# Hybrid trunk kernel: other order of projections inside the attention heads of layer 1, value projection one step later in layer 0, and waits on exponential and root kept only where they share a PSUM bank

## What is computed

```python
qh = (rms_norm(cq, g_mla_q) @ w_mla_qb).reshape(B, T, MLA_HEADS, MLA_NOPE + MLA_ROPE)   # 8 heads, 64 + 32
kvh = (rms_norm(ckv, g_mla_kv) @ w_mla_kvb).reshape(B, T, MLA_HEADS, MLA_NOPE + MLA_V)  # 64 of keys, 128 of values
f['gqa_q'] = rope_2d(rms_norm(gq.reshape(B, T, GQA_HEADS, GQA_HD), g_gqa_q), tabs_gqa)  # 8 heads of 128, 2 of keys
s = jnp.einsum('bqhgd,bshd->bhgqs', qblk, kf) * scale
pr = jax.nn.softmax(s, axis=-1)
out = jnp.einsum('bhgqs,bshe->bqhge', pr, vf)
f['gates'] = gates.reshape(B, T, N_BRANCH, D_MODEL)   # 3 x 1024 columns of h @ w_in
```

## Time and profile before

| | |
|---|---|
| median of 3 runs | 3745.88 us (3745.24 to 3748.95) |
| the profiled execution, its own time | 3743.77 us |
| its span, first to last instruction | 3741.9 us |
| mean granted TensorE clock | 0.938 of 2.4 GHz |
| TensorE busy, matmuls | 3305.7 us (88%) |
| TensorE busy, weight loads | 2786.6 us (74%) |
| VectorE, ScalarE, GpSimd busy | 1550.6, 1281.4, 477.3 us (41%, 34%, 13%) |
| DMA | 297.11 MB, 79 GB/s |

### The profile page before, as it was taken

The page is one execution under the profiler, slowest core; times in us unless marked ns, Lnnn a source line. Parts: engine busy times, 40 slices in busy tenths (PEclk is TensorE's granted clock), DMA queues, the critical chain, the costliest instruction groups (busy, mean ns, idle before and its releaser), DMA issues.

```text
span 3741.9 us, 50235 instructions
## 1 busy us (share of the span) xinstructions
PE 3305.7 (88%) x18696; PEld 2786.6 (74%) x18696; DVE 1550.6 (41%) x1997; ACT 1281.4 (34%) x1778; POOL 477.3 (13%) x340
## 2 busy tenths in 40 slices
PE   6788897999999988799999967988798999879998
PEld 4678776888888876588888746777677777758886
DVE  4455423544334433422222245653455344453334
ACT  3344332444333332221211223443344333433222
POOL 2011100111000000300000130220011001021001
PEclk8888898999999999899999978999899999989999
DMA  4111141111321123124233231212111321223332
GB/s 159 55 43 56 38 124 40 61 56 60 115 65 62 53 91 128 51 63 133 73 95 107 96 124 54 68 59 84 56 58 61 99 64 62 82 93 100 93 99 95
DMA packets 91434, 297.11 MB, mean 79 GB/s; under 512 B 10320, under 2 KB 16592, under 8 KB 91344
## 3 DMA queue, kind: packets, MB, share of 16 engines
q1 hardware_dynamic: 55872, 202.40, 17.1%
q10 hardware_dynamic: 35472, 93.49, 7.6%
HBM read 274.88 MB, written 20.97 MB: 79 GB/s over the span
## 4 chain that ended last, share of the span: by engine, by line
PE 40%; issue 9%; DVE 6%; ACT 3%; DMA 3%; POOL 1%; ACTq 0%; DVEq 0%; POOLq 0%
PE ps L1278 37%; DMA mraw<-in_wmod 2%; DVE prob L1001 1%; PE ps L1366 1%; DVE mx L838 1%; PE ps L1344 1%; POOL ptl L1260 1%; ACT pth L437 1%; DVE tmp L983 0%; DVE tmp L817 0%; ACT wh L384 0%; DVE wl L807 0%; DVE ptl L856 0%; DVE xz L1165 0%; DVE tmp L877 0%
## 5 line engine op out<-in xcount | busy, mean ns | idle before, releaser
L1278 PE MATMUL ps<-hh,wh 128*128 128x512 f32 x2768 | 835.0, 362 | 123.0 <-POOL hl L1242 64.0
L1278 PE MATMUL ps<-hl,wh 128*128 128x512 f32 x2768 | 823.1, 358 | 0.0
L1278 PE MATMUL ps<-hh,wl 128*128 128x512 f32 x2768 | 820.5, 357 | 0.0
L807 DVE TENSOR_TENSOR wl<-raw,wh 128x1024 fp32r<-128x1024 f32 x364 | 481.9, 1324 | 696.8 <-ACT wh L384 669.3
L1278 PEld LDWEIGHTS ps<-hh,wh 128*128 128x128 f32 x2768 | 457.7, 192 | 223.9 <-issue 59.0
L1278 PEld LDWEIGHTS ps<-hh,wl 128*128 128x128 f32 x2768 | 458.5, 192 | 78.5
L1278 PEld LDWEIGHTS ps<-hl,wh 128*128 128x128 f32 x2768 | 459.9, 193 | 73.6
L384 ACT ACTIVATE wh<-raw 128x1024 fp32r<-128x1024 f32 x364 | 382.8, 1052 | 245.9 <-PE ps L1278 202.6
L1278 PE MATMUL ps<-yh,wh 128*128 128x512 f32 (+1 forms) x1296 | 410.2, 371 | 37.4 <-DVE yl L1132 17.1
L1278 PE MATMUL ps<-yl,wh 128*128 128x512 f32 (+1 forms) x1296 | 397.8, 361 | 0.0
L1278 PE MATMUL ps<-yh,wl 128*128 128x512 f32 (+1 forms) x1296 | 397.4, 361 | 0.0
(11 more groups left out here) (176 smaller groups left out, 3729.3 us busy)
## 6 DMA issues: line engine op xcount, KB each, us to landing
raw<-in_stream SPq DMA_DIRECT2D x364, 512.0 KB, 3.6
mraw<-in_wmod ACTq DMA_DIRECT2D x80, 512.0 KB, 3.7
gspill<-prob ACTq DMA_DIRECT2D x24, 384.0 KB, 2.3
tmp<-gspill ACTq DMA_DIRECT2D x24, 384.0 KB, 3.1
early<-in_wmod SPq DMA_DIRECT2D x16, 512.0 KB, 15.0
dec<-in_dec ACTq DMA_DIRECT2D x8, 768.0 KB, 4.2
gspill<-side ACTq DMA_DIRECT2D x24, 256.0 KB, 2.2
tmp<-gspill ACTq DMA_DIRECT2D x24, 256.0 KB, 2.7
```

The source lines that it names most:

```text
L807: dve.tensor_tensor(wl[:, s, :], raw[:, s, :], wh[:, s, :].bitcast(F32), ALU.subtract).then_inc(sem("w_lo"), 1)
L1278: ins = pe.matmul(out, lhs[w], rhs[x](cols), start=start and n == 0, stop=stop and n == 2)
```

## The change

Six edits:

1. `mla_steps`: with six tiles the values are projected in step 5, not 4; with four tiles the gate comes in step 0 and the query in step 1, not the other way round.
2. `mla_order` is new: it gives the place of query, gate and key/value chunk in a head's three chunks (query, gate, pair with six tiles; gate, query, pair with four; without a gate or without a query 0, 0, 1). Waits for `product` and `free0` use it. ScalarE and VectorE split a head's second chunk in step 0 and its third in step 1 in either case; the rotary step follows the query projection by one step, the query's split by two.
3. `stream_of`: the last layer's latent heads have their gate chunk ahead of the query chunk.
4. TensorE waits for `y_lo` only ahead of the scores of tiles 0 and 2, not of tile 4.
5. PV waits for the exponential of tile min(n, 2), not min(n, nq-2). With four tiles this is the same number.
6. The wait for `v_std` moves from the end of `fill(2)` to ahead of the score of tile 3, and is gone from the projections of the first grouped-query head, which no score follows at once.

```diff
@@ mla_steps, mla_order @@
-    return (0, (1, 2), 3, 4) if nq == 6 else (0, (1,), 2, 3)
+    return (0, (1, 2), 3, 5) if nq == 6 else (1, (0,), 2, 3)
+def mla_order(nq, gated):
+    return ((0, 1, 2) if nq == 6 else (1, 0, 2)) if gated else (0, 0, 1)
@@ ScalarE, mla_head @@
                 q, gs, k, v = mla_steps(nt // P)
-                ck = c0 + 1 + gated
+                iq, ig, ik = mla_order(nt // P, gated and query)
                 def fill(n):
+                    if query and n == 0:
+                        split(at, c0 + 1)
+                    if query and gated and n == 1:
+                        split(at, c0 + 2)
                     if query and n == q:
-                        split(at, c0 + 1)
-                        act.wait_ge(sem("product"), at.v("chunk", c0 + 1))
+                        act.wait_ge(sem("product"), at.v("chunk", c0 + iq + 1))
...
-                    if query and gated and n == gs[0]:
-                        split(at, ck)
                     if gated and n == gs[-1]:
-                        gate_out(at, c0 + query, f0 + query, kg, nt)
-                    if query and n == 2:
+                        gate_out(at, c0 + ig, f0 + ig, kg, nt)
+                    if query and n == q + 2:
...
@@ VectorE, mla_head @@
-                    if query and n == q:
+                    if query and n == 0:
                         split(at, c0 + 1)
-                    if query and n == 1:
-                        dve.wait_ge(sem("free0"), at.v("free0", f0 + 1))
+                    if query and n == q + 1:
+                        dve.wait_ge(sem("free0"), at.v("free0", f0 + iq + 1))
                         cosine(at, MLA_NOPE)
                         sine(at, kp, MLA_NOPE)
-                    if query and gated and n == gs[0]:
+                    if query and gated and n == 1:
                         split(at, c0 + 2)
-                    if query and n == 2:
+                    if query and n == q + 2:
                         query_lo(at, kp, par, nt)
@@ TensorE, attend and values @@
-                        if n % 2 == 0 and c.has(n - 5):
+                        if n in (0, 2) and c.has(n - 5):
                             pe.wait_ge(sem("y_lo"), c.v("y_lo", n // 2 - 3))
+                        if n == 3 and std is not None:
+                            pe.wait_ge(sem("v_std"), std)
...
-                pe.wait_ge(sem("s_exp"), c.v("s_exp", min(n, c.nq - 2)))
+                pe.wait_ge(sem("s_exp"), c.v("s_exp", min(n, 2)))
@@ TensorE, mla_head and gqa_query @@
-                        project(at, c0, 0, f0, R[0], RKT, nt, whole)
+                        project(at, c0 + iq, 0, f0 + iq, R[0], RKT, nt, whole)
                     if gated:
-                        gate(at, c0 + query, f0 + query, gs, n, nt)
+                        gate(at, c0 + ig, f0 + ig, gs, n, nt)
...
-                    if query and n == 2:
-                        pe.wait_ge(sem("v_std"), at.v("v_std", kq + 1))
@@ TensorE, the loops @@
-                            attend(t, k, 1 - k, nt, head(t, 3 * k, nf * k, k))
+                            std = t.v("v_std", k + 1) if kind == "gqa" else None
+                            attend(t, k, 1 - k, nt, head(t, 3 * k, nf * k, k), std=std)
@@ stream_of @@
+            if h and layer == DEPTH - 1:
+                gate(h - 1)
             put(split_rope(w["w_mla_qb"][layer][:, h * MLA_QK:(h + 1) * MLA_QK], MLA_NOPE))
-            if h:
+            if h and layer < DEPTH - 1:
                 gate(h - 1)
```

More of the change, by code:

```diff
@@ L488, in fill @@
                     if query and n == v:
-                        plain(at, ck, 0, vh[:, par, :])
+                        plain(at, c0 + ik, 0, vh[:, par, :])
                 return fill
@@ L1313, in stats, with attend @@
                 ins.then_inc(sem("v_stat"), 1)
-            def attend(at, ka, par, nt, fill=lambda n: None, first=False, last=False):
+            def attend(at, ka, par, nt, fill=lambda n: None, std=None, first=False, last=False):
                 c = Tiles(at, ka, nt // P, first)
@@ L1392, in mla_head @@
                 q, gs, k, v = mla_steps(nt // P)
-                ck, fk = c0 + 1 + gated, f0 + 1 + gated
+                iq, ig, ik = mla_order(nt // P, gated and query)
+                ck, fk = c0 + ik, f0 + ik
                 s = at.slot(ck)
@@ L1500, in _ @@
                     pe.wait_ge(sem("v_lo"), at.v("v_lo", 1))
-                    attend(at, 0, 0, nt, head(at, c1, f1, 1), first=True)
+                    std = at.v("v_std", 2) if kind == "gqa_first" else None
+                    attend(at, 0, 0, nt, head(at, c1, f1, 1), std=std, first=True)
                 elif kind in ("mla", "gqa"):
```

## The result

The changed kernel takes 3720.26 us (median of six runs, 3716.8 to 3726.0); the kernel before took 3745.56 us beside it. The ratio is 0.9933, with a 95% interval of 0.9919 to 0.9946: 0.67% faster. The forecast was 3724. The profiled execution took 3716.8 us, with a span of 3715.0.

The account below looks back on a forecast made before the run. TensorE is busiest in all attention stages, so time is won only where it waits or runs at half clock. -15.6 - 1.1 + 6.5 - 1.3 - 10 = -21.5 from 3743.8 gives 3722.3, 3724 for the median; range 3708 to 3741.

Parts of the forecast that it names:

- forecast -15.6 and -1.1: Layer 0 latent: seven heads gain 15.6 us as values cover step 5's wait; last head's PV starts 1.1 us earlier.
- Rival (b): Layer 0 latent: value projection stays at half clock behind PV, +15 instead of -15.6 us, kernel 3755; chance 0.07.
- rival (d): Layer 0, step 4: the exponential is not what it waits for; partly true, 1.1 us, in the sum; no separate chance.
- forecast +6.5 and -1.3: Layer 1 latent, gate first: seven heads lose 0.95 us each, +6.5; last head's gate fills step 0's wait, -1.3.
- forecast -10: Layer 1 grouped-query: root waited for before score 3 gains 10 us net of half clock; bounds -15.5 and -6.
- -15.5 of the forecast: Layer 1 grouped-query: six heads' gain without the root wait, 15.5 us, before the half clock charge of +5.5.
- forecast 0: Layer 0 grouped-query: neither removed wait ends last, as a 4.3 us gate piece intervenes; 0 within 1 us.
- Rival (a): Layer 0 and 1 attention heads: half clock behind the waits takes the gain, no change, 3745; chance 0.12.
- Rival (c): Waits fall so little work is at half clock: layer 0 -3.5 a head, grouped-query -15, kernel 3710; chance 0.15.

Follow-up runs that it names:

- e5: e1 with PV of step 4 waiting for exp(4) again: 3738.99 us, ratio 0.9982.
- e1: Kernel before with layer 0's part alone: values in step 5, PV waiting for at most exp(2), no `y_lo` wait in step 4: 3727.24 us.
- e6: e1 with the values back in step 4, so that only the waits are cut: 3740.28 us, ratio 0.9989.
- e7: The changed kernel with the `y_lo` wait of step 4 put back: 3721.67 us, ratio 0.9937.
- e3: Kernel before with only the root's wait moved ahead of score 3: 3733.51 us, ratio 0.9974.
- e8: e4 with layer 0's split of the next weight chunk moved from step 3 to step 4, behind tile 1: 3708.98 us.
- e10: e4 with layer 1's grouped-query query halves made earlier: high half ahead of exp(3), low half ahead of reciprocal and scale: 3697.25 us.
- e11: e10 with layer 0's whole key block, copy and split, moved to step 4: 3676.83 us, ratio 0.9822.
- e4: The changed kernel with layer 1's latent order put back to query first: 3716.66 us, ratio 0.9930.

## Why the prediction was right

**Layer 0, latent (forecast -15.6 and -1.1; stage -17.1).** The mechanism is right, and so is the size of each term. Wait 4.63 (4.7 forecast); stretch 15.4 us (15.3 + 0.15); seven stretches 123.72 - 107.63 = -16.1; `ptl` unmoved at +4.74; PV at half clock and the projection at full. In the last head the wait fell from 5.02 to 3.86, -1.16. The sum hides two small errors that cancel: outside the stretches the seven heads got 1.2 us longer, and the last head got 2.2 us shorter and not 1.1. Rival (b) needed the value projection at half clock behind PV, and it ran at 1.00. Its argument, that the projection never brings the clock back and PV does, is not what the trace shows: before the change the clock fell during the projection and came back 6.8 or 10.2 us later, after the change 3.4 or 6.8 us later, and what ran meanwhile doesn't tell the heads apart. That exp(4) was worth something only with the values moved (e5 less e1: 10.5 us) is rival (d) in its right size: the shorter wait alone, e6, is nothing.

**Layer 1, latent (forecast +6.5 and -1.3; stage +7.1).** With T the transposes at 2375.96, keys at T+7.08 (7.05 forecast), exp(2) at T+9.03 (8.95), PV at T+10.07 (10.0), next head at T+19.88 (19.9). Heads 28.6 instead of 28.8. The wait at the head's start was 0.82, not 1.3, since TensorE was ready that much later; by the timeline the head's length hung on VectorE. Two terms were mis-sized. The last head, given -1.3, takes 44.3 us after 44.2: its step 0 wait of 3.16 us went, but the one in step 2 grew from 3.52 to 4.07, and TensorE was busy at half clock for 15.6 us of that head after 11.0. The seven heads were given +6.5 at 0.95 each; six of them grew by 4.6 in all, 0.76 each, and the first by 2.5, so that +7.0 is close to the forecast by luck.

**Layer 1, grouped-query (forecast -10; stage -12.2).** From the maximum's start to the next score 3.98 us (3.97), and no wait for the root. Six heads went from 205.25 to 192.05 us, -13.2. The term that was mis-sized is the half clock at the new place: 0.9 us in each of six heads was taken, +5.5; it came in two of six, 2 x 1.6 = 3.2. Without it the six heads would have given -16.4, near the -15.5 of the forecast. The last head is 1.2 us longer with the half clock behind its own wait, and the first 0.3 shorter: -12.2 in all. The wait was 2.4 us, not 2.9. The Trainium skill (TensorE: Matmul & The Clock Gate, "HAM oscillation — how this bites in real kernels") tells of a kernel that waits 3 to 5 us in every turn of its loop and is throttled again each time. The waits here are shorter, and the trace shows half clock behind some of them all the same: behind 2.75 to 2.85 us in five heads of six before, behind 2.35 to 2.44 us in two of six now.

**Layer 0, grouped-query (forecast 0).** -2.6 inside a spread of 3.6 between profiles. With the `y_lo` wait put back (e7) the stage takes 335.4 us, with the root's wait alone moved (e3) 332.8, both inside that spread too.

**The sum.** -21.5 was forecast against the profiled execution; it came to -27.0, of which -22.2 (-17.1, +7.1, -12.2) are in the three stages that the sum is about, close to the -21.5. The other -4.8 are the spread of the profiles and no merit of the forecast. Rival (a) happened in a third of the heads of layer 1, at no cost in the latent ones, and left the value projections of layer 0 alone. Rival (c), 3710, was reached by no part of the change, but by e8, e10 and e11: it needed shorter waits, and these hung on VectorE's queue.

## What to carry to other kernels

A wait may grow and the kernel still win: what counts beside the idle time is how much work runs at half clock behind it. Here two waits of 2.46 and 1.63 us became one of 4.63, and work at half clock fell from 64.9 to 27.4 us in seven heads. So read the granted clock window by window, not only the waits. Then ask what the releaser of the wait does just before: moving a weight split and a key copy behind the tile, and a query half ahead of a scale that it does not need, was worth 40 us here (e11 against e4), against 25 for the change itself. A gate piece that covers a chain is not free to fill another wait: in layer 1 two waits of 1.2 us became three of 2.1, 0.7 and 0.8.

## What was unexpected of the hardware

How long TensorE may wait before PV falls to half clock has no sharp edge in these runs. Behind waits of 3.40 (e8), 4.63 (the change) and 5.75 us (e5) PV ran at half clock, wholly or for most of its time in all heads but one of e8; behind 2.56 (e11) in three heads of seven, behind 2.44 (grouped-query, layer 1) in two of six, and behind the 2.10 and 0.68 around the keys in two of six. But behind the 2.46 us of the kernel before, in layer 0, the clock fell in all seven, so the length of the wait alone doesn't decide it. Where the fall lies matters too: before the change it came up to 2 us behind a wait of 2.46 us, and 6.8 or 10.2 us of work ran at 0.50; behind 4.63 us it came in the wait or at its end, and 3.4 to 5.6 us of work did. So the last microsecond of a wait can be worth more than itself: from e8 to e11 the wait ahead of PV fell by 0.84 us in each of seven heads, 5.9 in all, and the stage by 16.4. What else decides between two heads with the same wait stays open.
